# Attention scores: the causal mask of the diagonal block added by VectorE in PSUM instead of by a TensorE product with the identity

## The reference

```python
p_cmp = masked_softmax(s_cmp, cmp_mask)          # 15 compressed blocks
...
s = jnp.einsum("bqged,bqgnld->bqgenl", qb, ks) * scale     # selected blocks
m = (kpos <= tq[None, :, None, None, None])[:, :, :, None]
p = masked_softmax(s.reshape(s.shape[:4] + (-1,)), m.reshape(m.shape[:4] + (-1,)))
...
s = jnp.einsum("bqged,bkgd->bqgek", qb, kw) * scale        # sliding window
mw = (kp[None, :] <= tq[:, None]) & (kp[None, :] > tq[:, None] - WINDOW) & (kp[None, :] >= 0)
p = masked_softmax(s, mw[None, :, None, None, :])
...
o = g[..., 0:1] * o_cmp + g[..., 1:2] * o_slc + g[..., 2:3] * o_win
```

## Time and profile before

| what | value |
|---|---|
| runs, us | 2606.19, 2604.04, 2606.27 (median 2606.19) |
| the profiled execution, us | 2604.49 |
| its span, us | 2602.8 |
| granted TensorE clock, mean | 0.999 |
| busy share of the span: PE, DVE, ACT, POOL | 99%, 67%, 54%, 3% |
| attention stage | about 1652 to 1725 us of the span |

### The profile page before, as it was taken

One profiled execution on the slowest core, in us unless ns is written; L12 is line 12 of the kernel. 1 busy time (PEld: TensorE's weight loads), 2 busy tenths in 40 slices (PEclk: granted clock), 3 DMA queues, 4 the chain that ended last, 5 costly groups with the idle time before them and its releaser, 6 DMA issues.

```text
span 2602.8 us, 38974 instructions
## 1 busy us (share of the span) xinstructions
PE 2572.1 (99%) x14758; PEld 2236.0 (86%) x14758; DVE 1737.0 (67%) x2352; ACT 1396.4 (54%) x1911; POOL 68.3 (3%) x58
## 2 busy tenths in 40 slices
PE   7999999999999999999999999999999999999998
PEld 7999898888888888888888888888888888888887
DVE  4789966567755775576664666854577647764775
ACT  5588765456644554455544544654566535543554
POOL 2001210000000000000000000000000000000001
PEclk9999999999999999999999999999999999999999
DMA  6554444555555555555666566225655555555554
GB/s 219 169 179 146 130 132 164 192 195 190 192 192 188 187 193 193 188 185 181 202 208 196 170 184 193 66 70 186 214 194 185 189 192 194 187 188 192 192 174 166
DMA packets 238965, 465.70 MB, mean 179 GB/s; under 512 B 12558, under 2 KB 14206, under 8 KB 238718
## 3 DMA queue, kind: packets, MB, share of 16 engines
q1 hardware_dynamic: 237358, 461.77, 54.8%
q10 hardware_dynamic: 1488, 2.29, 0.3%
HBM read 461.94 MB, written 2.10 MB: 178 GB/s over the span
## 4 chain that ended last, share of the span: by engine, by line
PE 96%; DVE 1%; DMA 1%; ACT 1%; issue 0%; SPq 0%; ACTq 0%; DVEq 0%
PE bank L1882 33%; PE bank L1885 16%; PE bank L1919 10%; PE bank L1921 10%; PE bank L1920 10%; PE bank L2198 4%; PE bank L2199 4%; PE bank L2200 4%; PE bank L2367 1%; PE bank L2303 1%; PE bank L2243 1%; PE bank L2134 1%; DMA weight_raw<-in_ab_w_in 1%; PE bank L2348 0%; ACT weight_head L693 0%
## 5 line engine op out<-in xcount | busy, mean ns | idle before, releaser
L1197 DVE TENSOR_TENSOR weight_tail<-weight_raw,weight_head 128x2048 fp32r<-128x2048 f32 (+1 forms) x456 | 998.3, 2189 | 781.3 <-ACT weight_head L693 780.2
L693 ACT ACTIVATE weight_head<-weight_raw 128x2048 fp32r<-128x2048 f32 (+1 forms) x456 | 832.2, 1825 | 890.9 <-DMA weight_raw<-in_ffn_w_up 317.9
L1882 PE MATMUL bank<-norm_in,weight_head 128*128 128x512 f32 x3712 | 1167.5, 396 | 0.1
L1885 PEld LDWEIGHTS bank<-norm_in,weight_tail 128*128 128x128 f32 x3712 | 697.6, 188 | 164.2
L1885 PE MATMUL bank<-norm_in,weight_tail 128*128 128x256 f32 x3712 | 729.8, 278 | 0.0
L1882 PEld LDWEIGHTS bank<-norm_in,weight_head 128*128 128x128 f32 x3712 | 566.1, 189 | 1.4 <-issue 0.5
L1919 PE MATMUL bank<-weight_head,mixed 128*128 128x512 f32 x1088 | 425.1, 391 | 0.4 <-DVE weight_tail L1197 0.4
L1921 PE MATMUL bank<-weight_head,mixed 128*128 128x512 f32 x1088 | 423.7, 389 | 0.0
L1920 PE MATMUL bank<-weight_tail,mixed 128*128 128x512 f32 x1088 | 423.6, 389 | 0.0
L2198 PE MATMUL bank<-norm_in,weight_head 128*128 128x256 f32 x896 | 259.0, 289 | 3.4 <-DVE conf_pad L1459 1.3
L2199 PE MATMUL bank<-norm_in,weight_head 128*128 128x256 f32 x896 | 253.8, 283 | 0.0
(11 more groups left out here) (316 smaller groups left out, 1566.3 us busy)
## 6 DMA issues: line engine op xcount, KB each, us to landing
weight_raw<-in_ffn_w_up SPq DMA_DIRECT2D x176, 1024.0 KB, 5.0
weight_raw<-in_ffn_w_down SPq DMA_DIRECT2D x64, 1024.0 KB, 5.1
weight_raw<-in_cd_w_in SPq DMA_DIRECT2D x64, 1024.0 KB, 5.7
weight_raw<-in_ab_w_in SPq DMA_DIRECT2D x56, 1024.0 KB, 5.1
weight_raw<-in_ab_w_out SPq DMA_DIRECT2D x32, 768.0 KB, 4.3
weight_raw<-in_ffn_w_down SPq DMA_DIRECT2D x32, 768.0 KB, 4.4
weight_raw<-in_cd_w_out SPq DMA_DIRECT2D x32, 768.0 KB, 4.5
residual<-in_x SPq DMA_DIRECT2D x4, 512.0 KB, 5.6
```

What stands on the lines that cost most here:

```text
L693: act.activation(WHEAD[:, off % RING, 0:kt * CW], WRAW[:, off % RING, 0:kt * CW], ACT.Copy)\
L1197: dve.tensor_tensor(WTAIL[:, off % RING, 0:kt * CW], WRAW[:, off % RING, 0:kt * CW], WHEAD[:, off % RING, 0:kt * CW].bitcast(F32), ALU.sub ...
L1882: pe.matmul(bank[c][:, :], head, rhs[:, u * s.kt + k, :], start=u == 0 and k == 0, stop=False)
L1885: mm = pe.matmul(bank[c][:, 0:SEQ], tail, rhs[:, u * s.kt + k, 0:SEQ], start=False, stop=u == s.units - 1 and k == s.kt - 1)
```

## The change

The mask is kept as fp32, the copy of the identity goes, and L2304 goes. In `maxima`, VectorE first adds the mask in place to the diagonal block of both branches in the scores' bank, then does the compressed branch's addition, then waits for its own addition (`s_masked`) before the maximum.

```diff
@@ -262,8 +262,7 @@
         ONES = take("ones", [P, P], F32)
         TRI = take("tri", [P, P], F32)
         UST = take("ust", [P, P], F32)
-        IDENT_R = at("ident_r", places["tri"], [P, P], F32R)
-        MASK_R = at("causal", places["ust"], [P, P], F32R)
+        MASK = at("causal", places["ust"], [P, P], F32)
         RSTD = take("rstd", [P, SEQ], F32)
         STAT = take("stat", [P, SEQ], F32)
         SQ = take("squares", [P, SEQ], F32)
@@ -416,7 +415,7 @@
             "s_done", "s_read", "mx_ready", "p_ready", "pn_ready", "pt_done", "pt_read", "o_done", "o_read"))
         out_gained, fg_landed, out_read = sem("out_gained"), sem("fg_landed"), sem("out_read")
         store_ready = sem("store_ready")
-        tap1_mlp, mask_ready = sem("tap1_mlp"), sem("mask_ready")
+        tap1_mlp, mask_ready, s_masked = sem("tap1_mlp"), sem("mask_ready"), sem("s_masked")
         conf_halved, ysq_halved = sem("conf_halved"), sem("ysq_halved")
         vc_cleared, prob_cleared, early_cleared = sem("vc_cleared"), sem("prob_cleared"), sem("early_cleared")
         sel_copied, sel_ready, halves_done, halves_read = (sem(n) for n in (
@@ -651,9 +650,8 @@
                 pool.wait_ge(sel_copied, a + 1)
                 pool.affine_select(out=SEL[0:BROWS, a, :], in_=SEL[0:BROWS, a, :], compare_op=ALU.not_equal, fill=1.0,
                                    base=-(KVH * NBLK + a), pattern=[[0, KVH * NCMP]], channel_multiplier=1).then_inc(sel_ready, 1)
-            pool.tensor_copy(IDENT_R[:, :], IDENT[:, :]).then_inc(mask_ready, 1)
-            link(pool.memset(MASK_R[:, :].bitcast(F32), 0.0))
-            pool.affine_select(out=MASK_R[:, :], in_=MASK_R[:, :].bitcast(F32), compare_op=ALU.is_ge, fill=NEG,
+            link(pool.memset(MASK[:, :], 0.0))
+            pool.affine_select(out=MASK[:, :], in_=MASK[:, :], compare_op=ALU.is_ge, fill=NEG,
                                base=0, pattern=[[-1, P]], channel_multiplier=1).then_inc(mask_ready, 1)
             pool.wait_ge(kv_ready, 4 * 6 + 1)
             pool.memset(VCT, 0.0).then_inc(vc_cleared, 1)
@@ -1728,8 +1726,14 @@
                 scores = bank[4 + b][:, :].rearrange("p (r k) -> p r k", r=2)[:, :, 0:P * (t + 1)]
                 if n >= 5:
                     dve.wait_ge(pt_done, n - 2)
+                if n == 0:
+                    dve.wait_ge(mask_ready, 1)
                 dve.wait_ge(s_done, n + 1)
+                diagonal = scores[:, :, P * t:P * (t + 1)]
+                dve.tensor_tensor(diagonal, diagonal, MASK[:, :].unsqueeze(1).to_broadcast([P, 2, P]), ALU.add)\
+                   .then_inc(s_masked, 1)
                 dve.tensor_tensor(prob(n, 2, NCMP), bank[6 + b][:, 0:NCMP], CMPM[:, t, :], ALU.add).then_inc(s_read, 1)
+                dve.wait_ge(s_masked, n + 1)
                 dve.tensor_reduce(MX[:, 4 * b + 1:4 * b + 3], scores, AXX, ALU.max, negate=True).then_inc(mx_ready, 1)
                 dve.wait_ge(s_read, n + 1)
                 dve.tensor_reduce(MX[:, 4 * b:4 * b + 1], prob(n, 2, NCMP), AXX, ALU.max, negate=True).then_inc(mx_ready, 1)
@@ -2293,16 +2297,13 @@
                 if n == 0:
                     pe.wait_ge(vc_ready, 1)
                     pe.wait_ge(kv_ready, 4 * 6 + 1)
-                    pe.wait_ge(mask_ready, 2)
                 if n >= 2:
                     pe.wait_ge(s_read, n - 1)
                     pe.wait_ge(p_ready, 3 * (n - 1))
                 qh = ZX[:, 8 + h, t * P:(t + 1) * P]
                 nk = P * (t + 1)
                 dst = bank[4 + b][:, :].rearrange("p (r k) -> p r k", r=2)
-                pe.matmul(dst[:, :, 0:nk], qh, BC[:, 2 * g:2 * g + 2, 0:nk], start=True, stop=False)
-                pe.matmul(dst[:, :, nk - P:nk], IDENT_R[:, :], MASK_R[:, :].unsqueeze(1).to_broadcast([P, 2, P]),
-                          start=False, stop=True)
+                pe.matmul(dst[:, :, 0:nk], qh, BC[:, 2 * g:2 * g + 2, 0:nk], start=True, stop=True)
                 if n >= 3:
                     pe.wait_ge(pt_read, 2 * (n - 2))
                 pe.matmul(bank[6 + b][:, 0:NCMP], qh, KCR[:, g * NCMP:(g + 1) * NCMP], start=True, stop=True)\
```

## The result

The changed kernel takes 2611.60 us (median, 2609.49 to 2612.98), the kernel before 2605.73 us beside it (2604.04 to 2606.83): ratio 1.0021, interval 1.0014 to 1.0029. It is slower by 5.9 us; forecast were 5.0 and 2611.2.

What follows compares the result with a forecast made beforehand. The prediction took a closed cycle over VectorE and TensorE as the bound in steady heads, VectorE in series in the start-up. Its terms summed to +5.02 us, 2609.5 for the profiled execution, and 1.7 to the median gave 2611.2; range 2607 to 2616.

Steps and rivals of the forecast that it cites:

- L2304's worth, 0.12: Each removed TensorE product with the identity, one per item, saves 0.12 us by the modelled ends, not its row's 0.68.
- 12 products in the chain: Of the 32 removed products, the number said to count towards the time, beside 18 masks.
- The mask's price, 0.36: On VectorE, each item's maximum starts 0.36 us later because it waits for the mask addition.
- that rival: Writing the PSUM bank costs VectorE more: +5.6 to +11.3 us, so 2611.8 to 2617.5; chance 0.27.
- the forecast's own case: A mask price of 0.33 to 0.39 us, giving +4.5 to +5.6, so 2610.7 to 2611.8; chance 0.50.
- The extra 0.065: Possible added cost per mask on VectorE for PSUM, from the skill's fixed costs; would make the sum 6.2 us.
- The start-up, +2.16, less 0.24 ahead of it: Attention stage's start: masks of items 2 to 7 in series on VectorE, +2.16 us; items 0 and 1 save 0.24.
- Steady heads, +0.25 each: Ten heads, each an even and an odd item, 4.71 us long: each grows 0.25 us, +2.50 in all.
- The two cycles: In a steady head, one over VectorE and TensorE, one through ScalarE: next odd item at 1691.29 and 1691.30, a tie.
- The head with the weight tail, +0.72: The head where VectorE is full from the weight tail on: masks 10 and 11 add 0.72 us.
- The end, -0.12: Last items: masks 30 and 31 are covered by 1.3 us of waiting; item 31's removed product saves 0.12.
- Not slower: Rival: VectorE's 0.75 us idle per head swallows both masks and TensorE keeps all 3.8 us: 2602.4; chance 0.06.

Runs made afterwards that it cites:

- e1: Kernel before without the product with the identity and with no mask in its place: 2605.08 us against 2605.65, ratio 0.9997.
- e5: Changed kernel with the even item's reciprocals moved ahead of L1855's wait from item 6 on: 2608.84 us against 2605.66 for the kernel before, ratio 1.0012.
- e4: Kernel before with the mask on VectorE from item 8 on, on TensorE for items 0 to 7: 2608.51 us against 2605.65, ratio 1.0012.
- e2: Kernel before with the mask on VectorE for even items only: 2606.72 us against 2605.65, ratio 1.0004.
- e3: Kernel before with the mask on VectorE for odd items only: 2609.18 us against 2605.65, ratio 1.0015.
- e7: Kernel before with the even reciprocals moved as in e6 and the even masks on VectorE from item 12 on: 2604.91 us against 2605.66, ratio 0.9998.
- e6: Kernel before with the even item's reciprocals moved ahead of L1855's wait from item 6 on: 2603.92 us, ratio 0.9993.

## Why the prediction was right

- **The bound.** TensorE reads 99% busy and is not the bound of a steady head. e1 takes 3.8 us of products off it and gets 1.5; e5 moves one small VectorE operation and gets 0.21 a head.
- **L2304's worth, 0.12.** e1's head is 4.58 against 4.70, one product a head; right. The forecast's count of 12 products in the chain should read 13 (items 0 and 1, ten heads, item 31); its sum is added up term by term and holds.
- **The mask's price, 0.36.** By the trace the maximum starts 0.46 after the mask, where 0.45 was forecast from the dependent pair of the earlier trace rows, and used to start 0.09 after the compressed addition: 0.46 - 0.09 = 0.37. Where masks stand in series it comes to 0.39 each (2.33 / 6 in the start-up, 0.78 / 2 in the head with the weight tail). The mask lasts 0.42, as L1204, which writes SBUF: writing the bank costs no more, and that rival's cause falls. The time alone does not tell the two apart: +5.9 lies above the forecast's own case (+4.5 to +5.6) and inside that rival's +5.6 to +11.3; the rows decide it. The extra 0.065, an estimate from the fixed costs that the Trainium skill (Perfetto Trace Analysis, section Optimizing Scalar/DVE Operations) gives for PSUM and SBUF, is not seen for an output either.
- **The start-up, +2.16, less 0.24 ahead of it.** From the first mark to item 6's transposes it is 1670.07 - 1650.99 = 19.08 against 16.75, so +2.33. e4 puts both together at 2.04, against 1.92 forecast.
- **Steady heads, +0.25 each.** Measured 0.26 for the first and 2.45 / 9 = 0.27 for the others, in sum 2.71 against 2.50. The two cycles tie as worked out: the odd L2309 at 1688.83 ends at 1689.12, and the next odd mask starts 0.12 later, 0.34 behind L1859 at 1688.90. Which of the two holds the head, no run here tells: e5's move shortens both. e2 and e3 show which of the two masks is in the cycle.
- **The head with the weight tail, +0.72.** Measured 6.46 - 5.68 = 0.78.
- **The end, -0.12.** Measured -0.10; behind it no change shows that is larger than what runs differ by.
- **Not slower.** VectorE's idle time does swallow the even mask in a steady head (e2), and not the odd one (e3): the idle time is in the wrong place.

The sum of the stage is 5.48 against 5.02. The term that was sized a little low is the mask's price, and with it the start-up (0.17 of the difference), the ten steady heads (0.21) and the head with the weight tail (0.06). The rest of the 5.9 lies outside the stage and within what runs differ by. That the time, 2611.6, comes so near the forecast of 2611.2 is in part luck: the change was 0.85 larger than forecast, and the kernel before ran 0.46 below the median that the forecast started from. The forecast had put the change just under the 0.2% line; it lies just above.

## What to carry to other kernels

When an engine reads as fully busy, look for the place where it stands just behind another engine's last instruction; if a cycle runs over two engines, work removed from one counts only on the piece that lies in the cycle. Work added to the other counts there in full, and beside it not at all as long as no second cycle is nearly as long (e2, and e7 for the limit). Idle time elsewhere on an engine is no cover for work that must stand in the cycle. Moving an operation that has its inputs early out of the cycle can bring more than removing work that lies mostly off it: here 2.0 us of the stage (e6) against 1.5 (e1). And where the effect is near the spread of whole runs, measure the stage between two marks in the trace.

## What the runs showed of the hardware that was not expected

An addition by VectorE in place in a PSUM bank lasts 0.42 us for 128x256, no longer than one that writes SBUF (L1204, 0.42). The next operation, which needs nothing of it, starts 0.33 behind its start; the maximum, which needs its result, 0.46 behind it, with that operation in between, against 0.45 for the dependent pair that writes SBUF.
